# Last block: products and sums of the scanned states on GpSimd for seven of eight half groups, two readout terms instead of four

## The reference, cut to what matters

```python
bu_re = jnp.einsum('bsgc,gnc->bsgn', ug, bb_re)
bu_im = jnp.einsum('bsgc,gnc->bsgn', ug, bb_im)
# x[t] = a * x[t-1] + bu[t], a complex: |a| * exp(i * angle)
_, _, xr, xi = lax.associative_scan(combine, (ar, ai, bu_re, bu_im), axis=1)
y = (jnp.einsum('bsgn,gcn->bsgc', xr, c_re.astype(f32))
     - jnp.einsum('bsgn,gcn->bsgc', xi, c_im.astype(f32))).reshape(bsz, s, SSM_WIDTH)
y = y + d_skip.astype(f32) * uf
yg = jax.nn.gelu(y, approximate=False)
out = yg * jax.nn.sigmoid(yg @ w_glu.astype(f32) + b_glu.astype(f32))
```

## Time and profile before

| what | us |
|---|---|
| median of three runs | 1390.9 |
| the profiled execution, first to last instruction | 1388.9 |
| between the two | 2.0 |
| TensorE busy in it | 1368.8 |
| VectorE busy in it | 996.3 |
| ScalarE busy in it | 793.3 |
| GpSimd busy in it | 177.8 |

### The profile page before, as it was taken

The page is one execution under the profiler, slowest core; times in us unless marked ns, Lnnn a source line. Parts: engine busy times, 40 slices in busy tenths (PEclk is TensorE's granted clock), DMA queues, the critical chain, the costliest instruction groups (busy, mean ns, idle before and its releaser), DMA issues.

```text
span 1388.9 us, 20395 instructions
## 1 busy us (share of the span) xinstructions
PE 1368.8 (99%) x6833; PEld 1117.6 (80%) x6833; DVE 996.3 (72%) x1889; ACT 793.3 (57%) x1556; POOL 177.8 (13%) x323
## 2 busy tenths in 40 slices
PE   7999999999999999999999999999999999999998
PEld 6888888887887888889888888888888888877667
DVE  6978655559566755569766555599888666789976
ACT  6676644547665645548656554467665445675344
POOL 4100000000111000002000000001049992000000
PEclk9999999999999999999999999999999999999999
DMA  8534655555423755553336555545356556353132
GB/s 290 167 113 142 231 181 183 189 187 187 146 96 113 248 181 188 193 181 120 122 96 223 187 194 193 182 141 178 122 175 212 181 182 207 126 182 122 61 121 92
DMA packets 154389, 230.35 MB, mean 166 GB/s; under 512 B 7512, under 2 KB 103328, under 8 KB 154320
## 3 DMA queue, kind: packets, MB, share of 16 engines
q1 hardware_dynamic: 152352, 224.05, 48.4%
q0 software_dynamic: 1968, 5.43, 1.4%
HBM read 228.40 MB, written 1.05 MB: 165 GB/s over the span
## 4 chain that ended last, share of the span: by engine, by line
PE 90%; DVE 6%; ACT 2%; issue 1%; DMA 0%; SPq 0%; DVEq 0%; ACTq 0%
PE ps L2050 23%; PE ps L2052 23%; PE ps L2051 23%; PE ps L2056 3%; PE ps L2064 3%; PE ps L2060 3%; PE ps L2980 1%; DVE w_rest L1348 1%; PE ps L2328 1%; PE ps L2387 1%; DVE x L1411 1%; PE ps L2080 1%; ACT w_head L817 1%; PE ps L2894 1%; PE ps L2316 1%
## 5 line engine op out<-in xcount | busy, mean ns | idle before, releaser
L2050 PE MATMUL ps<-w_head,xt_head 128*128 128x512 f32 (+1 forms) x1200 | 471.4, 393 | 4.3 <-DVE w_rest L1348 2.5
L1348 DVE SCALAR_TENSOR_TENSOR w_rest<-w_raw,gain_t,w_head 128x512 fp32r<-128x512 f32 (+1 forms) x596 | 415.4, 757 | 74.7 <-ACT w_head L817 73.8
L817 ACT ACTIVATE w_head<-w_raw,gain_t 128x512 fp32r<-128x512 f32 (+1 forms) x596 | 375.4, 700 | 154.8 <-PE ps L2052 125.3
L2052 PE MATMUL ps<-w_head,xt_rest 128*128 128x512 f32 (+1 forms) x1200 | 461.1, 384 | 0.0
L2051 PE MATMUL ps<-w_rest,xt_head 128*128 128x512 f32 (+1 forms) x1200 | 460.2, 384 | 0.0
L2050 PEld LDWEIGHTS ps<-w_head,xt_head 128*128 128x128 f32 x1200 | 226.5, 189 | 49.9 <-issue 8.3
L2052 PEld LDWEIGHTS ps<-w_head,xt_rest 128*128 128x128 f32 x1200 | 226.2, 188 | 45.3
L2051 PEld LDWEIGHTS ps<-w_rest,xt_head 128*128 128x128 f32 x1200 | 226.8, 189 | 40.7
L1346 DVE TENSOR_TENSOR w_rest<-w_raw,w_head 128x1024 fp32r<-128x1024 f32 x124 | 153.4, 1275 | 82.2 <-ACT w_head L817 81.7
L817 ACT ACTIVATE w_head<-w_raw 128x1024 fp32r<-128x1024 f32 x124 | 124.7, 1053 | 98.2 <-PE ps L2052 96.8
L2050 PE MATMUL ps<-w_head,ht_head 128*128 128x512 f32 x320 | 124.9, 390 | 0.0
(11 more groups left out here) (493 smaller groups left out, 1543.5 us busy)
## 6 DMA issues: line engine op xcount, KB each, us to landing
w_raw<-in_ffn_w_gate_dram SPq DMA_DIRECT2D x88, 512.0 KB, 3.7
w_raw<-in_ffn_w_up_dram SPq DMA_DIRECT2D x88, 512.0 KB, 4.7
w_raw<-in_ffn_w_down_dram SPq DMA_DIRECT2D x88, 512.0 KB, 4.1
w_raw<-in_a_w_in_dram SPq DMA_DIRECT2D x48, 512.0 KB, 4.7
w_raw<-in_b_w_in_dram SPq DMA_DIRECT2D x24, 512.0 KB, 4.6
w_raw<-in_w_in_dram SPq DMA_DIRECT2D x24, 512.0 KB, 4.4
w_raw<-in_a_w_out_dram SPq DMA_DIRECT2D x16, 512.0 KB, 4.4
w_raw<-in_c_w_in_dram SPq DMA_DIRECT2D x10, 512.0 KB, 4.4
```

The source lines that it names most:

```text
L817: ins = act.activation(w_head[:, s, w], raw(u)[:, w], ACT.Copy, scale=1.0 if by is None else by)
L1348: ins = dve.scalar_tensor_tensor(w_rest[:, s, w], raw(u)[:, w], by, hd, ALU.mult, ALU.subtract)
L2050: pe.matmul(out_, hd, wh, start=first, stop=False)
L2052: return pe.matmul(out_, rt, wh, start=False, stop=last)
```

## The change

For h = 0 to 6, VectorE stops after the scans and signals `scanned`. GpSimd waits for it and makes six instructions of 128x512: four products with the tables and, new, a subtract and an add that combine them to xr and xi. It signals `xs_summed`. TensorE's `readout(h)` waits for that and makes two terms instead of four. Half group 7 stays as it was. Readouts 0 to 5 are moved to later places in TensorE's order, and `y_out(1)` and `y_out(2)` change places with `turned_out(4)` and `turned_out(6)` on VectorE.

```diff
+            def states_out(h):
+                t_, z0, z1, e_ = s5_piece[h]
+                cs, sn = half_tiles(h // 2, h % 2)
+                pool.wait_ge(scanned, h + 1)
+                pool.tensor_tensor(t_, z0, cs, ALU.mult)
+                if h:
+                    pool.wait_ge(y_ready, h)
+                step(pool.tensor_tensor(e_, z1, sn, ALU.mult))
+                pool.tensor_tensor(z0, z0, sn, ALU.mult)
+                step(pool.tensor_tensor(z1, z1, cs, ALU.mult))
+                pool.tensor_tensor(t_, t_, e_, ALU.subtract)
+                pool.tensor_tensor(z0, z0, z1, ALU.add).then_inc(xs_summed, 1)
...
+            for h in range(7):
+                states_out(h)
...
+                    if h < 7:
+                        last.then_inc(scanned, 1)
+                        return
                     step(last)
                     dve.tensor_tensor(t_, z0, cs, ALU.mult)
...
                 def readout(h):
-                    pe.wait_ge(xs_done, h + 1)
                     k, half = h // 2, h % 2
+                    pe.wait_ge(*((xs_summed, h + 1) if h < 7 else (xs_done, 1)))
...
+                    terms = ((0, re_cos), (1, re_sin)) if h < 7 else ((0, re_cos), (0, im_sin), (1, re_sin), (1, im_cos))
+                    for j, (c, z) in enumerate(terms):
...
+                half_unit(6, 0)
                 pe.wait_ge(turn_used, tr + 3)
                 readout(0)
-                half_unit(6, 0)
...
-                readout(1)
                 half_unit(8, 0)
                 pe.wait_ge(qk_normed, 1)
                 turn_group(tok[:, :, 0:512], 0, 2)
                 pe.wait_ge(qk_normed, 2)
                 turn_group(tok[:, :, 512:1024], 0, 3)
+                readout(1)
...
-                readout(2)
                 half_unit(10, 0)
                 weights_turned(0)
                 pe.wait_ge(turn_used, tr + 6)
                 turn_group(tok[:, :, 512:1024], 1, 7)
+                readout(2)
...
                 half_unit(11, 1)
-                readout(3)
                 pe.wait_ge(in_out, 12)
                 project(0)
+                readout(3)
                 weights_turned(1)
...
                 driven(5)
-                readout(4)
...
                 project(1).then_inc(unit_used, 1)
+                readout(4)
...
                 o_turn(0)
-                readout(5)
                 pe.wait_ge(t_done, pair + 3)
                 scores(3)
                 pe.wait_ge(o_there, 1)
                 values(2)
+                readout(5)
```

More of the change, by code:

```diff
@@ L384, in build @@
         s5_in2 = sem("s5_in2")
+        scanned = sem("scanned")
+        xs_summed = sem("xs_summed")
         p_in = sem("p_in")
@@ L1656, in dilated @@
                 turned_in(4)
+                turned_out(4)
                 y_out(1)
-                turned_out(4)
                 turned_in(5)
@@ L1665, in dilated @@
                 gated(2)
+                turned_out(6)
                 y_out(2)
-                turned_out(6)
                 gated(3)
@@ L2324, in readout @@
                     re_cos, re_sin, im_cos, im_sin = s5_piece[h]
-                    for j, (c, z) in enumerate(((0, re_cos), (0, im_sin), (1, re_sin), (1, im_cos))):
+                    terms = ((0, re_cos), (1, re_sin)) if h < 7 else ((0, re_cos), (0, im_sin), (1, re_sin), (1, im_cos))
+                    for j, (c, z) in enumerate(terms):
                         for i in range(2):
                             r_ = slice(64 * half + 32 * i, 64 * half + 32 * i + 32)
-                            last = pe.matmul(ps[r_, 6, 0:TOK], c_t[:, c, k, r_], z[:, i, :], start=j == 0, stop=j == 3, skip_group_check=True)
+                            last = pe.matmul(ps[r_, 6, 0:TOK], c_t[:, c, k, r_], z[:, i, :], start=j == 0, stop=j == len(terms) - 1, skip_group_check=True)
                     last.then_inc(y_ready, 1)
```

## The result

The changed kernel takes 1403.5 us (median of four runs, 1402.8 to 1404.7) where the kernel before takes 1390.8 in the same session: a ratio of 1.0091, interval 1.0077 to 1.0106. It is slower by 12.7 us. The prediction said slower, 1395.2, with 1399 as its upper end; the time lies outside. The profiled execution spans 1403.0 us, 14.1 more than the one of before.

A forecast was written before the change was run, and what follows sets the result against it. TensorE, busy 99% of the span, was taken as the bound. Terms: -7.1 + 0.3 + 4.3 + 1.8 + 1.4 + 0.4 + 0.5 + 2.7 = +4.3 us; 1388.9 + 4.3, with 2.0 around it, 1395.2 us; range 1387.5 to 1399.

The forecast's parts named there:

- seven readouts shorter: On TensorE, eight records less at 0.108 us each, 0.87 us per readout; seven readouts give -6.1 us.
- readout 0: TensorE waits 0.3 us there: GpSimd ends its first set near 1249.1, TensorE is there at 1248.8.
- turning of q and k: New TensorE wait of 4.3 us, because `qk_norm` on VectorE ends late, held by GpSimd; bounds 0 to 5.5.
- `weights_turned(0)`: TensorE waits 1.8 us (1.4 to 2.7) for `exp(0)`, since readout 2 no longer covers it.
- `project(0)`: TensorE waits 1.4 us for `out_of(5)`, since readout 3 now stands behind; said not to depend on VectorE.
- `values(1)` and `scores(3)`: TensorE waits 0.4 and 0.5 us for the copies of `spread_out(1)`, which readout 4 had hidden.
- readout 5: TensorE waits 2.7 us for a side chain of 15.5 us plus some 1.8 of holds; 0.9 without holds.
- What GpSimd takes (6.9 us): GpSimd's six instructions per half group: 4 x 1.04 + 2 x 1.29 + 0.2 = 6.9 us; VectorE took 2.5.
- What GpSimd does to VectorE (0.8 us per product): VectorE instructions with SBUF operands alone are held 0.8 us per GpSimd product, 1.1 per add or subtract.
- Rival 2: VectorE's tiny instructions slip through and half the holds fall into idle time: +1.0, 1391.9 us; chance 0.17.
- Rival 1: No hold that matters: GpSimd runs beside VectorE, no `qk_norm` wait, -2.5, 1388.4 us; chance 0.13.
- a case in which VectorE falls behind: `rest` of units 8 to 10 comes late, delay adds two or three more microseconds, 1398 us; chance 0.13.

The follow-up runs named there:

- The experiment with all waits filled: Changed kernel with unread matmuls put into four of TensorE's waits (q/k turning, `weights_turned(0)`, `project(0)`, readout 5): 1400.7 us.
- the first experiment: Changed kernel's order with the work of the kernel before (four products on VectorE, four readout terms, GpSimd idle): 1395.5 us, ratio 1.003.
- the kernel with GpSimd idle: Changed kernel without GpSimd's six instructions per half group; two-term readouts wait only for the scans, states not turned back: 1388.6 us, ratio 0.9983.
- the kernel with one wait filled: Changed kernel with 18 unread matmuls of 128x512 in front of the first turning of q and k: 1403.55 us.
- the kernel with private tiles: GpSimd-idle kernel plus six GpSimd instructions of the same shape per half group on tiles of its own, nobody waiting for them: 1397.7 us.

## Why the prediction was wrong

The direction and the reason stood: it is slower because GpSimd and VectorE take turns, because GpSimd's own results come late, and because moved readouts uncover waits. The size did not. Term by term, in us:

| term | predicted | changed kernel |
|---|---|---|
| seven readouts shorter | -6.1 | -6.1 |
| old wait at readout 5 gone | -1.0 | -1.0 |
| readout 0 | +0.3 | +1.1 |
| turning of q and k | +4.3 | +4.9 |
| `weights_turned(0)` | +1.8 | +1.6 |
| `project(0)` | +1.4 | +2.5 |
| `values(1)` and `scores(3)` | +0.9 | +1.0 |
| readout 5 | +2.7 | +3.6 |
| TensorE at the lower clock | none | +2.8 and +1.7 |
| sum | +4.3 | +12.1 |

The sum is against 14.1 between the two profiled spans and 12.7 between the medians. Of the 14.1, 0.9 is there long before the changed block: GpSimd's load of the gains starts at 26.21 us in the profile after, and at 25.29 in that of before. So 1.1 of 13.2 us are in no term; the order alone has 0.7 such us, with no GpSimd in the block.

**The step that was left out.** No line of the prediction asks what TensorE does after a wait. It forecast one idle time of 4.3 us inside a stretch where the engine had been full, and gave the work behind it its old durations. The readout behind it took 1.93 us where two terms take 1.06, and seven of the twelve products behind that ran at half their pace. The experiment with all waits filled prices this, together with the work behind readout 5, at 2.8 us net. With that term the forecast would have been 1398, still 5.5 us short; the rest of the miss is in the sizes below.

**What GpSimd takes (6.9 us).** The step chose the wrong row: 1.04 us from a product whose operand is of another form, where the adds in the same group at 1.29 were the nearer row (two full tiles). With 1.27 for each a set is 7.7 us. The holds on GpSimd itself come on top. The first set, beside `rest`, took 9.8 us (1240.82 to 1250.64), where the prediction's times for readout 0 come to 9.3, and readout 0 waits 1.1 us in place of 0.3. For readout 5 the prediction took the undisturbed 6.9; that set took 8.6 us (1324.99 to 1333.58), with instructions of 1.60 and 1.71 us beside VectorE's. Of these 1.7 us VectorE made up 0.7, by doing its part in 9.7 us where 10.4 were reckoned, and the wait is 0.9 longer.
The Trainium skill (GPSIMD Engine Reference, Engine selection) puts GpSimd at about half of VectorE's speed for two inputs. Here it is 1.27 against 0.69 us, a ratio of 1.8, nearer to the page than to the 1.5 of my choice.

**What GpSimd does to VectorE (0.8 us per product).** Right in kind, a little small. Four quarters cost 3.1 us more, not 2.4: the prediction's own row had 5.86 for 2.73, but the step counted three holds of 0.8. It did so for both sets, so `qk_norm` ended 1.5 us later than forecast (without the 0.9 that the profile was late before the block); TensorE itself came 0.8 us later, by readout 0, and the two waits at the turning are 4.9 us in place of 4.3. The tiny instructions cost 3.2 us more for the three GpSimd instructions that were left, where the step said 3.0. Rival 2, in which they slip through, is refuted by three rows of 1.2 to 1.3 us.

**`project(0)`: "it does not depend on VectorE".** This sentence was false. It holds with GpSimd idle (1.4 us in two experiments), but the last transfer out of PSUM stands behind `exp(1)` on ScalarE, and `exp(1)` behind a 128x4 instruction that GpSimd's sum held for 1.1 us. I had followed the wait one step back and not two.

**What was right.** `weights_turned(0)`, `values(1)` and `scores(3)` came within 0.2 us, and the first experiment shows them with no GpSimd in play. For `weights_turned(0)` the reason was partly wrong: the prediction added some 0.4 us for a `peak(0)` made late by GpSimd, but the wait is 1.6 us with and without GpSimd. Rival 1, no holds, was worked out at 1388.4, and the kernel with GpSimd idle takes 1388.6; that is near by chance, since the rival's sum has 0.9 us at readout 5 that this kernel doesn't have.

**The range.** Its upper end came from a case in which VectorE falls behind, which didn't happen. All cases priced waits and none the work behind them, so they shared the missing term, and no mixture of them could reach 1403. The experiments split the 12.7 us otherwise: order +4.4, shorter readouts and no products on VectorE -6.9, GpSimd's presence +9.1, waiting for its results +5.8; they add to 12.4.

## What to carry to other kernels

An idle engine isn't free room when its instructions and those of a full one take turns: count each of its instructions as a hold on the full engine (here 0.8 to 1.1 us for one of 1.27), also for the smallest instruction there, and find who waits for that one. A wait that a change puts into the bounding engine has two prices, its length and the work behind it at a lower clock; look at the granted clock behind such a wait before the second is counted as nothing. And where a step is moved later to give a helper time, price the order alone first: here it cost 4.4 us of the 6.9 that the shorter readouts could give.

## What was not expected of the hardware

- A product on GpSimd of 128x512 costs 1.26 us with two full tiles and 1.04 with a spread column.
- Three of ten instructions of 128x32 on VectorE took 1.20 to 1.28 us beside GpSimd, for 0.18 to 0.19 alone; one of 128x4 took 1.31 for 0.17, and in another kernel, where it began between two sums of GpSimd, 0.20.
- TensorE's granted clock fell from 1.00 to 0.50 behind waits of 4.4 and 3.6 us inside a busy block. Behind a wait of 2.5 us in the changed kernel it stayed at 1.00, but it fell behind one of 1.9 in the kernel with one wait filled, and `project(0)` took 5.40 us for 3.70 behind one of 2.1 in the kernel with private tiles. The length of the last wait alone doesn't tell. What else does stays open; no run was made for it.
- Filling one wait with useless products gained 2.8 us on the spot and nothing at the end (1403.55 and 1403.5 us).
- Of the order's own 4.4 us, 0.9 is not in any wait that the trace shows; 0.4 of it stands at the turning of q and k, and the rest stays open.
